# Three of 256 row gathers issued as two parts each, in a fused two-block forward pass

## The reference, cut to what matters

```python
def token_chunk(xc):                       # 128 tokens
    q = (xc @ w_q).reshape(128, 8, 2, half)
    s = einsum("thpd,hpnd->thpn", q, subkeys)
    ...
    top_s, top_pos = lax.top_k(cand_s, 16)
    e = take_along_axis(cand_i, top_pos, axis=-1)
    g = softmax(top_s)
    a = gelu(einsum("td,thkd->thk", xc, w_down[e]))
    return einsum("thk,thkd->td", g * a, w_up[e])
```

## Time and profile before

| | us |
|---|---|
| median of 3 runs | 1357.02 |
| lowest and highest of them | 1354.96, 1357.57 |
| the profiled execution, its time | 1354.06 |
| the profiled execution, its span | 1352.2 |
| busy PE / DVE / ACT / POOL | 1212.1 / 931.4 / 531.8 / 291.5 |

### The profile page before, as it was taken

The page is one execution under the profiler, slowest core; times in us unless marked ns, Lnnn a source line. Parts: engine busy times, 40 slices in busy tenths (PEclk is TensorE's granted clock), DMA queues, the critical chain, the costliest instruction groups (busy, mean ns, idle before and its releaser), DMA issues.

```text
span 1352.2 us, 17522 instructions
## 1 busy us (share of the span) xinstructions
PE 1212.1 (90%) x6474; PEld 886.0 (66%) x6474; DVE 931.4 (69%) x1828; ACT 531.8 (39%) x955; POOL 291.5 (22%) x261
## 2 busy tenths in 40 slices
PE   9999999999999999999998999898778777777775
PEld 8999998899988899998774555454223232223222
DVE  6865748876664676467587777777776776776655
ACT  4843236445533446735533332233222222222312
POOL 0000000000000000000024544554444444544420
PEclk9999999999999999999999999999999999999999
DMA  7553235545565654447669999999999999999994
GB/s 277 187 184 128 94 119 214 190 165 187 181 223 187 218 187 158 153 159 280 264 278 379 419 419 420 420 419 420 419 421 420 419 420 419 420 419 420 420 420 191
DMA packets 55788, 396.76 MB, mean 293 GB/s; under 512 B 6304, under 2 KB 6304, under 8 KB 8352
## 3 DMA queue, kind: packets, MB, share of 16 engines
q0 software_dynamic: 36864, 268.45, 48.0%
q1 hardware_dynamic: 17136, 119.42, 25.1%
q10 hardware_dynamic: 1712, 7.87, 1.5%
HBM read 394.67 MB, written 1.05 MB: 293 GB/s over the span
## 4 chain that ended last, share of the span: by engine, by line
PE 57%; DMA 29%; DVE 6%; ACT 5%; issue 2%; SPq 0%; POOL 0%; DVEq 0%; ACTq 0%; POOLq 0%
DMA R<-experts,IDX 28%; PE ps L541 25%; PE ps L1094 11%; PE ps L624 10%; PE ps L591 3%; PE ps L553 3%; DVE JUNK L2333 1%; DVE w_lo L1634 1%; ACT w_hi L1144 1%; PE ps L944 1%; PE ps L740 1%; ACT DIAG L1509 1%; PE ps L728 1%; DMA XF<-xT 1%; PE ps L662 1%
## 5 line engine op out<-in xcount | busy, mean ns | idle before, releaser
L1094 PE MATMUL ps<-R,DIAG 128*128 128x512 f32 x1020 | 477.8, 615 | 118.5 <-ACT DIAG L1509 118.0
L1094 PEld LDWEIGHTS ps<-R,DIAG 128*128 128x128 f32 x1020 | 188.6, 194 | 386.6 <-issue 194.5
L2494 POOL DMA_INDIRECT R<-experts,IDX x256 | 290.2, 1133 | 545.9 <-PE ps L1094 310.1
L2333 DVE CUSTOM_DVE_ANT_0 JUNK<-R,XN 128x1024 f32<-128x1024 f32 x256 | 313.7, 1225 | 130.4 <-DMA R<-experts,IDX 127.9
L1634 DVE TENSOR_TENSOR w_lo<-raw,w_hi 128x1024 fp32r<-128x1024 f32 x206 | 242.7, 1220 | 101.2 <-ACT w_hi L1144 97.8
L1144 ACT ACTIVATE w_hi<-raw 128x1024 fp32r<-128x1024 f32 x206 | 206.0, 1050 | 85.1 <-DMA raw<-weights 85.1
L541 PE MATMUL ps<-opC_lo,w_hi 128*128 128x256 f32 x544 | 154.7, 284 | 2.1 <-DVE MB L1848 1.0
L541 PE MATMUL ps<-opC_hi,w_hi 128*128 128x256 f32 x544 | 153.9, 283 | 0.0
L541 PE MATMUL ps<-opC_hi,w_lo 128*128 128x256 f32 x544 | 153.9, 283 | 0.0
L1501 ACT ACTIVATE act_d<-dots,rst 128x2 f32<-128x2 f32 (+1 forms) x130 | 38.3, 295 | 268.4 <-DVE dots L2333 268.1
L1509 ACT ACTIVATE DIAG<-con,coef 128x128 f32<-128x128 f32 x255 | 88.6, 394 | 113.2 <-DVE coef L2343 111.8
(11 more groups left out here) (362 smaller groups left out, 1678.6 us busy)
## 6 DMA issues: line engine op xcount, KB each, us to landing
raw<-weights SPq DMA_DIRECT2D x104, 1024.0 KB, 4.8
PQW<-weights SPq DMA_DIRECT2D x6, 1024.0 KB, 9.7
R<-experts,IDX POOLq DMA_INDIRECT x256, 33.0
LNR<-rows ACTq DMA_DIRECT2D x3, 1024.0 KB, 4.9
XF<-xT SPq DMA_DIRECT2D x2, 512.0 KB, 6.0
raw<-weights SPq DMA_DIRECT2D x2, 512.0 KB, 6.5
MEM<-mem ACTq DMA_DIRECT2D x1, 1024.0 KB, 7.5
XR<-x ACTq DMA_DIRECT2D x1, 1024.0 KB, 5.0
```

The source lines that it names most:

```text
L1094: mm = pe.matmul(psum[:, 4 + 2 * m + n, :], DIAG[:, k, :], rows_[:, D + n * 512:D + (n + 1) * 512], start=(it % 8 == 0 and k == 0), stop=True,
L2333: dve.tensor_tensor_reduce(out=JUNK[:, :], in0=rows_[:, 0:D], in1=XN[:, it // 8, :], scale=1.0, scalar=0.0, op0=ALU.mult, op1=ALU.add, acc ...
L2494: pool.indirect_dma_start(out=R[u][:, :], out_offset=None, in_=experts, in_offset=bass.IndirectOffsetOnAxis(ap=IDX[:, it, k:k + 1], axis=0 ...
```

## The change

Gathers 63, 127 and 191 (the last pick of iterations 3, 7 and 11) are each issued as two indirect DMAs into the same buffer: rows 0 to 119, and rows 120 to 127. The second takes its eight row numbers from a new small tile `REST_IDX`, where they stand in partitions 0 to 7. SP copies them there from partitions 120 to 127 of `IDX`, once `idx_ready` says that they are written; POOL waits for that copy (`rest_in`) between the two parts. Both parts add 16 to the buffer's semaphore, so `NTH` counts such a gather twice.

```diff
+        PARTED, REST = (63, 127, 191), 120
...
-            _uses[u] = _uses.get(u, 0) + 1
+            _uses[u] = _uses.get(u, 0) + (2 if n in PARTED else 1)
...
+        REST_IDX = small("REST_IDX", [P, 8], U32)
...
+        rest_in = sem("rest_in")
...
+            for i, n in enumerate(PARTED):
+                it, k = n // TOPK, n % TOPK
+                sp.wait_ge(idx_ready, it + 2)
+                if i:
+                    sp.wait_ge(rest_in, 16 * i)
+                sp.dma_start(REST_IDX[0:P - REST, i:i + 1], IDX[REST:P, it, k:k + 1]).then_inc(rest_in, 16)
 
             sp.wait_ge(fin_y, 1)
...
+                    whole = REST if n in PARTED else P
                     pool.indirect_dma_start(
-                        out=R[u][:, :], out_offset=None, in_=experts,
-                        in_offset=bass.IndirectOffsetOnAxis(ap=IDX[:, it, k:k + 1], axis=0)
+                        out=R[u][0:whole, :], out_offset=None, in_=experts,
+                        in_offset=bass.IndirectOffsetOnAxis(ap=IDX[0:whole, it, k:k + 1], axis=0)
                     ).then_inc(row_in[u], 16)
+                    if n in PARTED:
+                        i = PARTED.index(n)
+                        pool.wait_ge(rest_in, 16 * (i + 1))
+                        pool.indirect_dma_start(
+                            out=R[u][REST:P, :], out_offset=None, in_=experts,
+                            in_offset=bass.IndirectOffsetOnAxis(ap=REST_IDX[0:P - REST, i:i + 1], axis=0)
+                        ).then_inc(row_in[u], 16)
```

## The result

The kernel with the change takes 1376.11 us (median of 4 runs, 1372.03 to 1379.48) against 1355.99 us before (median of 4, 1353.84 to 1357.57): +20.1 us, ratio 1.0148, 95% interval 1.0133 to 1.0164. It is slower by seven times what a measurement can tell, where 1350.2 was forecast, and it lies above the range. The profiled execution took 1376.06 us with a span of 1374.0, 21.8 more than the span before.

What follows compares the result with a forecast made beforehand. The second half was taken as a DMA-bound stream of row gathers, ending with one late engine alone for 7.7 us. Sparing it gave 1357.0 - 6.8 = 1350.2 us, other terms 0; range 1348.0 to 1358.2.

Steps and rivals of the forecast that it cites:

- point 1: Row dealing in the three parted gathers: the late engine is spared 24 rows, last landing 6.8 to 7.5 us earlier.
- The second half: Spared engine is the late one, all three times: 1350.2 us, own range 1348 to 1351.5; chance 0.62.
- the lone stretch: End of the gather stream: one engine working alone for about 7.7 us, until 1341.3; it should shrink to about a microsecond.
- 24 rows against a lag of 24.6: Rows spared, 7.5 us, set against the late engine's lag at stream end; cited for the forecast case.
- Point 2: After the stream: all later landings come earlier, DVE and PE follow, so the gain reaches the end; at most 7.7 us.
- The tail: Fixed work behind the last landing, to the kernel's end at 1352.2: 10.3 us, taken to stay.
- Points 3 and 4: POOL's three more issues, and SP's index copies with POOL's wait for them: all hidden, cost 0 each.
- Point 5: Landing: semaphore wants 32 for the three gathers, DVE waits for the later part; 48 more 4-byte completions, cost 0.
- The source of the lag: Between 740 and 1342 us: ten 16 KB packets on q8, some 10 us of one engine, would make the lag.
- The slower rival: Parts dealt to fewer engines, 24 more rows on a loaded engine: +7.5 us, 1364.5; chance 0.09.
- the rotating rival: Shares rotate, sparing three different engines: 1355.1 if the late one is among them, else 1357.6; chance 0.14.
- the three benign cases: Late engine spared (0.62), nothing moves or wrong engine spared (0.15), shares rotate (0.14): faster or at most about 1358.0 us.

Runs made afterwards that it cites:

- e3: Kernel before, with gathers 63, 127 and 191 issued as rows 0 to 119 only, the other eight rows not fetched: 1374.35 us, ratio 1.0134.
- e6: Kernel before, with only rows 32 to 95 of gathers 63, 127 and 191 issued, the rest left out: 1351.55 us, ratio 0.9972.
- e4: Kernel before, with gathers 63, 127 and 191 each issued as two parts of 64 rows: 1375.75 us, ratio 1.0142.
- e1: Kernel before, plus only SP's index copies and POOL's waits, the three gathers issued whole: 1355.17 against 1355.46 us, ratio 0.9998.
- e7: Kernel before, with gathers 63, 127 and 191 each issued as parts of 124 and 4 rows: 1399.95 us (one run), +44.9 us.
- e14: Kernel before, with only rows 36 to 99 of gathers 63, 127 and 191 issued, the rest left out: 1361.47 us, ratio 1.0048.
- e10: Kernel before, with gathers 63, 127 and 191 issued as rows 32 to 95, 0 to 31, then 96 to 127: 1365.94 us, ratio 1.0078.

## Why the prediction was wrong

- **The step that failed is point 1, in two halves.** The first half took the price of a row, 0.3125 us, from whole gathers and kept it whatever rows a transfer has. A row cost about twice that for all engines, in a stretch of some 8 to 10 us around each parted gather, and that is the 15.1 us in the windows. e3 shows it with the 120 rows alone, e6 shows the price kept where the placing is kept.
- **The second half** had the spared engine be the late one. It was not: the lone stretch grew from 7.7 to 11.5 us. 24 rows against a lag of 24.6 was a coincidence of numbers that I read as evidence. It had its rows each time, and it slowed in the dip of the others and again in its own. At the third dip its shares took 5.0 and 5.2 us in the dip of the others, then 2.5 and 2.5, then 4.7 for its own share of gather 191. That makes 7.4 us lost where the stream lost 5.7; at the second dip it lost 7.0 against 5.2, and these two differences, 3.5 us, are most of the 4.
- **The length of a dip.** A displaced gather is in flight 2.5 us on each engine, plus the time by which the fifteen are apart, 2.2, 3.0 and 2.9 us just ahead of the three dips. So much of the full-rate stream, done at half rate, loses as much again: 4.7, 5.5 and 5.4. Measured: 4.2, 5.2 and 5.7. This estimate, made with the result at hand, would explain e4's miss as well.
- **Point 2** (the gain reaches the end) had nothing to carry, but its form held for the loss: the 20.4 us at the last landing all reached the end. The tail was not quite fixed, 11.7 us where it was 10.3, by the clock.
- **Points 3 and 4 held.** POOL had no wait on the copies; the second part cost 0.90 to 1.61 us to issue, and gather 64 was issued 2.50 us behind 63 where it was 2.22 (e1 measures the copies and waits at 0). The copy of 32 bytes took SP 4.3 us of waiting, within 0 and 8.8.
- **Point 5 held** in its cost, with the landing of the second parts late for the same reason as all rows; it counted 48 more packets of 4 bytes, and there are 96.
- **The source of the lag** was put on q8's packets of 16 KB. The trace before the change points to q14's of 8 KB. From 850 us on nine of them, from 850.2 to 1326.5, are each followed by a gather row of 0.96 or 0.97 us in place of 0.31. Each time, within 5 us, the last engine is about 1 us further behind the first, from 2.3 us to 11.0 in all. So the lag very likely comes from fetched instructions and says nothing of rows; no run takes these packets away.
- **Two small misreadings**, on which nothing rests: DVE works 70 to 77 us of every 100, and the rate stands at 419 to 421 from the 23rd slice on, about 744 us.
- **The rivals.** The slower rival had the right sign and the wrong mechanism. It looked for rows piled on fewer engines; by e6 and e14 what counts is where the rows go, and a pile at the receiving side is the likely reason. As a mechanism it does exist, in e7. Of the rotating rival e7 shows how many engines a part gets; no run shows how the start moves on. It too priced rows at one price only. I gave the three benign cases 0.91 because all were worked out at one row price. The missing bound was: what if the rate itself is not kept.

## What stays open

The number of the late engine, and whether it can be relieved without displaced writes. A share of four rows on each of 15 engines in its own place would leave 68 rows whose parts are displaced again; e10 prices such parts at 3 to 4 us a gather, against 1.25 to 2.5 us to be had. No version that fetches all rows beat the kernel before. Why displaced shares slow all 16 engines, those with whole gathers too, is open as well.

## What to carry to other kernels

A saturated stream of gathers like this one can depend on where each engine writes. Here parts with another number or another start of rows cut the rate of the whole stream to about half for some 5 us and more, unless the rows fell as in e6. Before one splits or shortens a transfer in a saturated stream, ask where each engine will write, and look at the rate, not at the DMA share, which stayed at 1.0 here. And a lag of one engine read off the last windows is real, but it is not evidence of which rows that engine holds.

## What was not expected of the hardware

- Displaced shares slowed all 16 engines to about 210 GB/s together, not only those that hold one: in e7 four engines had the long shares, and the rate stood at 219 to 238 for 16 us.
- Four partitions of shift (rows 36 to 99 in place of 32 to 95) cost 10 us over three gathers.
- A split of 64 and 64 rows, even in every count, costs as much as 120 and 8: +20.3 and +20.1 us.
